# Router of a mixture-of-experts encoder layer: the four best by match-replace on padded rows, ranks offset in the rank matrix, gates and residual products at another place

## The reference, cut to what matters

```python
def moe_ffn(h, w_router, b_router, w_gu, b_gu, w_down, b_down):   # T = 256 tokens
    t = h.reshape(T, D)
    logits = (t @ w_router + b_router)                  # T x 32
    top_val, top_idx = lax.top_k(logits, 4)
    gates = jax.nn.softmax(top_val, axis=-1)
    ...                                                 # tokens sorted by expert
    def expert_block(args):                             # each expert over its tokens
        gu = xb @ w_gu[e] + b_gu[e]                     # 1024 -> 2048
        g, u = jnp.split(gu, 2, axis=-1)
        g = jnp.minimum(g, 7.0); u = jnp.clip(u, -7.0, 7.0)
        act = g * jax.nn.sigmoid(1.702 * g) * (u + 1.0)
        return act @ w_down[e] + b_down[e]              # 1024 -> 1024
    ...                                                 # times gate, summed by token
# reference: x = x + token_mixer(...); h = rmsnorm(x, norm2_g)
#            x = x + moe_ffn(h, ...);  return rmsnorm(x, final_g)
```

## Time and profile before

| | us |
|---|---|
| median of the runs | 1162.61 |
| lowest, highest | 1161.68, 1163.89 |
| the profiled execution, its time | 1161.16 |
| its span (first to last instruction) | 1159.4 |
| PE busy in it | 1085.6 (94%) |
| DVE busy in it | 378.7 (33%) |
| ACT busy in it | 233.7 (20%) |

### The profile page before, as it was taken

One profiled execution on the slowest core, in us unless ns is written; L12 is line 12 of the kernel. 1 busy time (PEld: TensorE's weight loads), 2 busy tenths in 40 slices (PEclk: granted clock), 3 DMA queues, 4 the chain that ended last, 5 costly groups with the idle time before them and its releaser, 6 DMA issues.

```text
span 1159.4 us, 13119 instructions
## 1 busy us (share of the span) xinstructions
PE 1085.6 (94%) x5379; PEld 497.7 (43%) x5379; DVE 378.7 (33%) x669; ACT 233.7 (20%) x370; POOL 0.2 (0%) x4
## 2 busy tenths in 40 slices
PE   5998999999999999999998989898989898999987
PEld 5997889833333333333333323333333333323332
DVE  6996798533122221222212121221221212112112
ACT  5388853110111111111101111111110101011102
POOL 0000000000000000000000000000000000000000
PEclk9999999989999999999999999999999999999999
DMA  8543236999999999999999999999999999999996
GB/s 351 186 173 142 77 132 278 419 407 382 423 384 429 427 426 430 428 428 430 427 430 427 428 430 428 429 428 427 430 427 428 430 428 430 428 427 428 428 427 262
DMA packets 33054, 439.95 MB, mean 379 GB/s; under 512 B 3808, under 2 KB 3936, under 8 KB 6272
## 3 DMA queue, kind: packets, MB, share of 16 engines
q1 hardware_dynamic: 32544, 438.53, 90.1%
q10 hardware_dynamic: 480, 0.99, 0.2%
HBM read 438.46 MB, written 1.05 MB: 379 GB/s over the span
## 4 chain that ended last, share of the span: by engine, by line
PE 62%; DMA 31%; DVE 3%; SPq 2%; ACT 1%; issue 1%; DVEq 0%
DMA slot<-in_w_gu_dram 26%; PE ps L1343 25%; PE ps L1047 12%; PE ps L1352 10%; DMA slot<-in_w_down_dram 5%; PE ps L1315 5%; PE ps L1296 3%; PE ps L1401 2%; SPq L352 2%; PE ps L1310 1%; PE ps L1102 1%; DVE slot_r L631 1%; PE ps L1145 1%; PE ps L1274 1%; PE ps L1166 1%
## 5 line engine op out<-in xcount | busy, mean ns | idle before, releaser
L1343 PE MATMUL ps<-slot,lru 128*64 128x512 f32 x880 | 198.5, 595 | 20.6 <-DMA slot<-in_w_gu_dram 20.2
L1352 PE MATMUL ps<-slot,lru 128*64 128x512 f32 x896 | 208.3, 600 | 7.3 <-DMA slot<-in_w_down_dram 7.1
L1343 PE MATMUL ps<-slot,qT 128*64 128x512 f32 x880 | 200.4, 597 | 14.0 <-DMA slot<-in_w_gu_dram 14.0
L992 DVE COPY lru<-ps 128x512 f32<-128x512 f32 x32 | 22.1, 692 | 337.2 <-PE ps L1343 337.2
L1343 PEld LDWEIGHTS ps<-slot,lru 128*64 128x64 f32 x880 | 63.0, 137 | 151.8 <-issue 113.8
L1343 PEld LDWEIGHTS ps<-slot,qT 128*64 128x64 f32 x880 | 61.3, 136 | 147.9 <-issue 133.2
L1352 PEld LDWEIGHTS ps<-slot,lru 128*64 128x64 f32 x896 | 57.8, 136 | 113.3 <-issue 92.6
L559 ACT ACTIVATE lru<-ps 128x512 f32<-128x512 f32 x32 | 19.1, 598 | 410.9 <-PE ps L1343 410.9
L975 DVE TENSOR_SCALAR lru<-sq,x_sb,small 128x64 f32<-128x64 f32 x64 | 17.2, 312 | 252.5 <-PE ps L1296 252.5
L1047 PE MATMUL ps<-wide_r,slot_r 128*128 128x256 f32 x492 | 66.2, 286 | 0.2 <-DVE slot_r L631 0.2
L1315 PE MATMUL ps<-lru 128*128 128x512 f32 x136 | 65.5, 605 | 0.9 <-DVE lru L1027 0.9
(11 more groups left out here) (213 smaller groups left out, 856.5 us busy)
## 6 DMA issues: line engine op xcount, KB each, us to landing
slot<-in_w_gu_dram SPq DMA_DIRECT2D x110, 2048.0 KB, 34.0
slot<-in_w_down_dram SPq DMA_DIRECT2D x54, 2048.0 KB, 33.6
wide<-in_w_gu_dram SPq DMA_DIRECT2D x15, 2048.0 KB, 34.5
slot<-in_pre_dram SPq DMA_DIRECT2D x14, 2048.0 KB, 8.2
wide<-in_w_down_dram SPq DMA_DIRECT2D x8, 2048.0 KB, 35.3
slot<-in_w_down_dram SPq DMA_DIRECT2D x8, 512.0 KB, 30.4
slot<-in_w_lru_dram SPq DMA_DIRECT2D x2, 1024.0 KB, 13.5
wide<-in_w_gu_dram SPq DMA_DIRECT2D x2, 1024.0 KB, 14.8
```

Of the source, the lines that this page charges most:

```text
L992: nc.vector.tensor_copy(gu_sb[:, 0:BANK], ps[:, 4, :]).then_inc(gu_v, 1)
L1343: ins = nc.tensor.matmul(ps[64 * side:64 * side + 64, 4 + b, :], xgT[i % 2][:, k, :], rows[r][:, o:o + BANK], start=(k == 0), stop=(k == K ...
L1352: ins = nc.tensor.matmul(ps[64 * side:64 * side + 64, bank, :], actT[(i - 1) % 2][:, k, :], w[:, r, side * BANK:(side + 1) * BANK], start= ...
```

## The change

- **Mask.** The logits have four more columns (`NL` = 36), which hold 3.0e38. The four largest values of a row are these, and the next four of the sorted eight (`top8[:, t, 4:8]`) are the chosen experts' logits. `match_replace` replaces all eight in a copy (`left`) by -3.0e38; the mask is where `left` differs from `logit`. This is the new `top_mask(t)`, which also makes the negative maximum. `top_experts(t)` keeps positions, floats and `hot`, and moves behind both tiles' ranks.
- **Ranks.** The first rank matrix is the upper-triangular ones minus 4096 times the identity, so the product has the offset in it; `first_ranks` is one addition and the selection matrix. The fill of `rank_col` with -1 moves up to where DVE waits for the mixer, and `rank_col` and `gate` have tiles of their own.
- **PE's order.** `residual_in_bank(0)` moves behind `gather_tile(1)`; `residual_in_bank(1)` moves behind `gathered_transposes(0)`; `ranks(0)` stands ahead of all of `logits(1)`; the gate transposes move into step 0, between `gate_up(0, 0, 0)` and `gather(1)`.
- **Gates.** The product with `hot` and its sum stand behind `scale_gathered(0, 0)`; one column block of gates is kept instead of five, and a step reads it at `n & 31`.

```diff
+NL = NE + TOPK
+HUGE = 3.0e38
...
-                nc.scalar.activation(ex4[:, t, :], top8[:, t, 0:TOPK], ACT.Exp, bias=nmax[:, t:t + 1],
+                nc.scalar.activation(ex4[:, t, :], top8[:, t, TOPK:2 * TOPK], ACT.Exp, bias=nmax[:, t:t + 1],
...
+            nc.vector.memset(logit[:, :, NE:NL], HUGE).then_inc(logits_padded, 1)
...
-            nc.vector.tensor_copy(tri[:, :, :], sq[:, 1:3, :]).then_inc(tri_ok, 1)
+            nc.vector.scalar_tensor_tensor(out=tri[:, 0, :], in0=ident, scalar=-FAR, in1=upper, op0=ALU.mult,
+                                           op1=ALU.add).then_inc(tri_ok, 1)
+            nc.vector.tensor_copy(tri[:, 1, :], ones).then_inc(tri_ok, 1)
+            dve.wait_ge(logits_padded, 1)
+            link(nc.vector.memset(rank_col[:, :, :], -1.0))
...
+            def top_mask(t):
+                link(nc.vector.match_replace(left[:, t, :], top8[:, t, :], logit[:, t, :], -HUGE))
+                nc.vector.tensor_tensor(mask_b[:, t, :], left[:, t, 0:NE], logit[:, t, 0:NE], ALU.not_equal
+                                        ).then_inc(mask_ok, 1)
+                nc.vector.tensor_scalar(nmax[:, t:t + 1], top8[:, t, TOPK:TOPK + 1], -1.0, None,
+                                        ALU.mult).then_inc(top_ok, 1)
...
             def top_experts(t):
                 link(nc.vector.max_index(idx_u[:, t, :], top8[:, t, :], logit[:, t, :]))
                 link(nc.vector.tensor_copy(idx_f[:, t, :], idx_u[:, t, :]))
                 link(nc.vector.tensor_tensor(hot[:, t], slotno[:, 0:NE].unsqueeze(1).to_broadcast(four),
-                                             idx_f[:, t, 0:TOPK].unsqueeze(2).to_broadcast(four), ALU.is_equal))
-                link(nc.vector.tensor_reduce(mask[:, t, :], hot[:, t].rearrange("p k e -> p e k"), AX.X, ALU.add))
-                nc.vector.tensor_copy(mask_b[:, t, :], mask[:, t, :]).then_inc(mask_ok, 1)
-                nc.vector.tensor_scalar(nmax[:, t:t + 1], top8[:, t, 0:1], -1.0, None, ALU.mult).then_inc(top_ok, 1)
+                                             idx_f[:, t, TOPK:2 * TOPK].unsqueeze(2).to_broadcast(four), ALU.is_equal))
...
             def first_ranks(t):
                 dve.wait_ge(rank_ps, t + 1)
-                link(nc.vector.scalar_tensor_tensor(out=ranked[:, t, :], in0=ps[:, 4 + t, 0:NE], scalar=FAR,
-                                                    in1=mask[:, t, :], op0=ALU.add, op1=ALU.mult))
-                link(nc.vector.tensor_scalar(rank_col[:, t, 0:NE], ranked[:, t, :], -FAR, None, ALU.add))
+                link(nc.vector.tensor_scalar(rank_col[:, t, 0:NE], ps[:, 4 + t, 0:NE], FAR, None, ALU.add))
...
             top_values(0)
+            top_mask(0)
             transposed_copy(1)
             inverse_variance(ssum[:, 1:2], T + 2)
-            link(nc.vector.memset(rank_col[:, :, :], -1.0))
-            top_experts(0)
             first_ranks(0)
             top_values(1)
-            top_experts(1)
+            top_mask(1)
             first_ranks(1)
+            for t in range(T):
+                top_experts(t)
...
             link(nc.vector.tensor_tensor(g4, ex4, einv.unsqueeze(2).to_broadcast([P, T, TOPK]), ALU.mult))
+            scale_gathered(0, 0)
             link(nc.vector.tensor_tensor(hotg, hot, g4.unsqueeze(3).to_broadcast([P, T, TOPK, NE]), ALU.mult))
-            link(nc.vector.tensor_reduce(gate, hotg.rearrange("p t k e -> p t e k"), AX.X, ALU.add))
-            nc.vector.tensor_copy(gate_col[:, :, 0:NE], gate).then_inc(mask_ok, 1)
...
-            scale_gathered(0, 0)
+            nc.vector.tensor_reduce(gate, hotg.rearrange("p t k e -> p t e k"), AX.X, ALU.add).then_inc(mask_ok, 1)
...
             for r in range(1, ROUNDS):
-                nc.vector.tensor_scalar(rank_col[:, :, r * NE:(r + 1) * NE], ranked, -FAR - CAP * r, None,
+                nc.vector.tensor_scalar(rank_col[:, :, r * NE:(r + 1) * NE], rank_col[:, :, 0:NE], -float(CAP * r), None,
                                         ALU.add).then_inc(cols_ok, 1)
-                nc.vector.tensor_copy(gate_col[:, :, r * NE:(r + 1) * NE], gate).then_inc(cols_ok, 1)
             dve.wait_ge(gateT_ps, 1)
...
+                e = column(n if isinstance(n, int) else n & (NE - 1))
                 for t in range(T):
                     nc.vector.tensor_scalar(sel_gate[:, t, o:o + CAP], slotno[:, 0:CAP], rank_col[:, t, column(n)],
-                                            gate_col[:, t, column(n)], ALU.is_equal, ALU.mult).then_inc(sgate_ok, 1)
+                                            gate[:, t, e], ALU.is_equal, ALU.mult).then_inc(sgate_ok, 1)
...
             second_transposes(1)
-            residual_in_bank(0)
-            logits(1, range(4))
             ranks(0)
-            logits(1, range(4, KD))
+            logits(1, range(KD))
...
                 gate_up(n, i, 0)
+                if first:
+                    gate_transposes()
                 if not last:
                     gather(n + 1)
...
             gather_tile(1).then_inc(xg_ps, 1)
+            residual_in_bank(0)
+            gathered_transposes(0)
             residual_in_bank(1)
-            gathered_transposes(0)
-            pe.wait_ge(mask_ok, T + 1)
-            for t in range(T):
-                ins = nc.tensor.transpose(ps[0:NE, 6, t * P:(t + 1) * P], gate[:, t, :], ident)
-            ins.then_inc(gateT_ps, 1)
             step(0, 0, True)
```

More of the change, by code:

```diff
@@ L144, in encoder_layer @@
         NCOL = (ROUNDS + 1) * NE
[L145 to L148, removed]
+        tflat = x_sb[:, 0, :]
+        rank_col = sb("rank_col", [P, T, NCOL])[:, :, :]
+        gate = sb("gate", [P, T, NE])[:, :, :]
+        logit = scratch(T * NL).rearrange("p (t e) -> p t e", t=T)
+        left = tflat[:, 640:640 + T * NL].rearrange("p (t e) -> p t e", t=T)
         top8 = tflat[:, 64:80].rearrange("p (t k) -> p t k", t=T)
@@ L155, in encoder_layer @@
         hotg = tflat[:, 384:640].rearrange("p (t k e) -> p t k e", t=T, k=TOPK)
-        mask = tflat[:, 640:704].rearrange("p (t e) -> p t e", t=T)
         mask_b = tflat[:, 835:867].bitcast(bf16).rearrange("p (t e) -> p t e", t=T)
-        gate = tflat[:, 704:768].rearrange("p (t e) -> p t e", t=T)
-        ranked = tflat[:, 768:832].rearrange("p (t e) -> p t e", t=T)
         cmax, rnd, rnd2 = tflat[0:1, 832:833], tflat[0:1, 833:834], tflat[0:1, 834:835]
@@ L892, in top_values @@
                 dve.wait_ge(rstd_ok, 2 + t)
-                link(nc.vector.scalar_tensor_tensor(out=logit[:, t, :], in0=ps[:, 4 + 2 * t, 0:NE],
+                link(nc.vector.scalar_tensor_tensor(out=logit[:, t, 0:NE], in0=ps[:, 4 + 2 * t, 0:NE],
                                                     scalar=rstd[:, t:t + 1], in1=brt[:, :], op0=ALU.mult, op1=ALU.add))
                 link(nc.vector.max(top8[:, t, :], logit[:, t, :]))
+            def top_mask(t):
[4 more added lines that the diff above has]
+                                        ALU.mult).then_inc(top_ok, 1)
             def top_experts(t):
@@ L900, in top_experts, with value, scale_gathered @@
                 link(nc.vector.tensor_tensor(hot[:, t], slotno[:, 0:NE].unsqueeze(1).to_broadcast(four),
[L901 to L904 removed]
+                                             idx_f[:, t, TOPK:2 * TOPK].unsqueeze(2).to_broadcast(four), ALU.is_equal))
             def first_ranks(t):
                 dve.wait_ge(rank_ps, t + 1)
[L908 to L910 removed]
+                link(nc.vector.tensor_scalar(rank_col[:, t, 0:NE], ps[:, 4 + t, 0:NE], FAR, None, ALU.add))
                 nc.vector.tensor_scalar(sel_next[:, t, :], slotno[:, 0:CAP], rank_col[:, t, 0:1], rstd[:, t:t + 1],
                                         ALU.is_equal, ALU.mult).then_inc(sel_ok, 1)
+            def value(v):
+                return v if isinstance(v, int) else dve.snap(v)
+            gain2 = cst[:, C_G2:C_G2 + KD].rearrange("p (h k) -> p k h", h=2)
+            def scale_gathered(n, i):
+                dve.wait_ge(xT_ps, value(n + 1))
+                nc.vector.tensor_tensor(xgT[i % 2].rearrange("p (h k) n -> p k h n", h=2),
+                                        ps[:, 7, :].rearrange("p (k h n) -> p k h n", k=KD // 2, h=2),
+                                        gain2.unsqueeze(3).to_broadcast([P, KD // 2, 2, CAP]),
+                                        ALU.mult).then_inc(xg_ok, 1)
             for n in range(3):
@@ L964, in _ @@
             nc.vector.tensor_copy(gateT, ps[0:NE, 6, 0:TOK].rearrange("p (t n) -> p t n", t=T)).then_inc(sg_ok, 2)
-            dve.wait_ge(cols_ok, 2 * (ROUNDS - 1))
+            dve.wait_ge(cols_ok, ROUNDS - 1)
+            dve.wait_ge(mask_ok, T + 1)
             def column(n):
@@ L1363, in down, with gate_transposes @@
                 ins.then_inc(chunk_used[4 + j], 1 + AHEAD if isinstance(n, int) and n == 1 else 1)
+            def gate_transposes():
+                pe.wait_ge(mask_ok, T + 1)
+                for t in range(T):
```

(2 more changed lines are left out.)

13 lines of the change are left out of this document (2 added, 11 removed).

## The result

| | before | after |
|---|---|---|
| median of 22 runs each, us | 1161.00 | 1163.57 |
| lowest and highest, us | 1158.50, 1164.48 | 1161.26, 1169.91 |
| profiled execution, its span, us | 1159.4 | 1162.8 |

The ratio of after to before is 1.0021, with a 95% interval of 1.0011 to 1.0031: the change costs 2.4 us (1.3 to 3.6). The forecast was 1163.6 us within 1161.1 to 1165.5, and "within 0.2%" with a chance of 79%. The time is the forecast one, but by luck, by two errors that cancel almost wholly: before is 1161.0 over 22 runs, not the 1162.6 of the three runs at hand, and the shift is 2.4 us, not 1.0. At 0.21% it lies just outside the 0.2%, and its interval of 0.11% to 0.31% reaches to both sides of that bound.

The account below looks back on a forecast made before the run. PE was taken to set the pace to 341.01 us, then the weight transfers; -1.55 + 0.91 + 1.34 + 0.35 = +1.05 us at `gather(1)` gave 1163.6 us on the median, range 1161.1 to 1165.5.

Parts of the forecast that it names:

- The frame: From step 0 to the issue at 341.01 PE sets the pace, then transfers; a `gather(1)` shift reaches the end unchanged.
- The mask's worth: Second tile, DVE line 893 to `gather_tile(1)`: shorter mask and ranks take 1.95 us in place of 3.10.
- `gather_tile(1)` starts 1.55 us earlier: In the router: earlier second-tile logits and the shorter mask start the second gather at 234.8 in place of 236.33.
- the clock term: Around the start of step 0: PEclk's low stretch stays where it was, step 0 starts further into it, 0.35 us more.
- the sign of a first `gate_up` that starts 0.4 to 1 us earlier: Start of step 0: a residual product directly ahead of `gate_up`, which starts that much before 241.96.
- The exposed residual product: Between the gathered transposes and the first `gate_up`: a residual product now stands there, 0.91 us more.
- The wait in step 0: Between the first `gate_up` and `gather(1)`: PE stands for gate transposes, DVE's copy and selection, 1.34 us.
- The sum: At `gather(1)` in step 0: -1.55 + 0.91 + 1.34 + 0.35 = +1.05 us, shifting the end alike.
- the second rival: In the router or step 0: more dense work at low clock, 3.3 us more of it, +2.7 in all, 1165.3; 15%.
- the first rival: In the router: shorter gaps keep the clock up, `gather(1)` comes 1.3 us earlier, 1161.3 us; 17%.
- The median to start from: Whole kernel before: the forecast started from 1162.6 us, the median of three runs that spread over 2.2 us.

Follow-up runs that it names:

- f: The kernel before with only the gate transposes moved into step 0, between the first `gate_up` and `gather(1)`; ratio to before 1.0014 (1.0005 to 1.0024).
- j: The kernel before with two unused 256-column products added in PE's stand-stills, ahead of `ranks(1)` and `gather_tile(1)`; ratio to before 0.9995 (0.9983 to 1.0007).
- e: The changed kernel with one unused residual-shaped product added between the second tile's transposes and `ranks(0)`; ratio to before 1.0001 (0.9986 to 1.0015).
- b: The changed kernel with PE's order of before and gates made ahead of the scaling, leaving the mask part; ratio to before 0.9988 (0.9978 to 0.9999).
- c: The changed kernel with both residual products back at their old places, gate transposes still in step 0; ratio to before 1.0007 (0.9994 to 1.0020).
- h: b with the first residual product cut in two halves, one between `ranks(1)` and the second gather; ratio to before 0.9973 (0.9959 to 0.9987).
- a: The changed kernel with DVE's `select(1)` ahead of the copy that waits for the gate transposes; ratio to before 1.0015 (1.0002 to 1.0028).
- d: The kernel before with only the residual products moved as in the change; ratio to before 1.0033 (1.0016 to 1.0050).

## Why the prediction was right, and where it was off

**The frame held.** PE sets the pace up to the issue at 341 us and the transfers behind it do from there on: a shift of `gather(1)` arrives in that issue unchanged, in all thirteen traces, and at the end of the span to 0.2 us in ten of them. The range held the time.

**The mask's worth held**: 1.95 us were worked out from DVE's line 893 to `gather_tile(1)`. In after it is 1.01 to the mask, 0.92 from `ranks(1)` (236.68) to 237.60, and 0.05 of signal, 1.98. The replacement took 0.18 us, as the search of the earlier trace rows. The prediction also set these rows against the Trainium skill, "VectorE: DVE Perf Modes", section on the TRN2 errata, and took from its table a fixed cost of 58 cycles. The text below that table says itself that the row under-predicts and that the measured fixed term is about 150 cycles. As an estimate from that figure 32 columns take 190 ns, and there the rows of 0.17 to 0.19 us agree.

**"`gather_tile(1)` starts 1.55 us earlier" failed.** From the start of the stretch it is 9.28 us after against 9.52 before: 0.24 earlier. The step that went wrong is the clock term: "if the low stretch stays where it was", 0.35 us. I took the low stretch to stay where it was, and so let the second tile's logits and `gather_tile(0)` run at full clock. They did not: the logits took 2.83 us from 232.02 in place of 1.9, about 0.9 more, and `gather_tile(0)` held up `ranks(1)` by 0.74 us, from 235.94 to 236.68. Against that, the logits began 0.3 us sooner than I had them. 1.55 - 0.9 - 0.74 + 0.3 is 0.21, the 0.24 within rounding. By this the sign of a first `gate_up` that starts 0.4 to 1 us earlier failed too: it starts 15.76 us into the stretch after against 15.15 before, 0.61 later.

**The exposed residual product** was put at 0.91 us. From `gather_tile(1)` to `gate_up` it is 5.63 us before and 6.48 after: 0.85.

**The wait in step 0** was put at 1.34 us, and in the change as a whole with 0.35 us of clock. From `gate_up` to `gather(1)` it is 3.73 before and 4.99 after: 1.26, since the clock was back sooner than I had it in after; f has 1.25 against the first profile of before and 1.50 against the second, whose `gate_up` ran at full clock as in f. The term is right to 0.2 us and the 0.35 us did not come.

**The sum**: -0.24 + 0.85 + 1.26 = +1.87 us in the profiles in place of +1.05, and 2.4 us (1.3 to 3.6) in the times. The difference is the clock. This is the second rival, which had 15%: it named an earlier fall, with the missing dense product as its cause, and had 3.3 us more of low clock, where 3.4 came. It put the price at 1.65 us over the forecast; against the forecast's own terms it took 0.8 us, since part of the low stretch lay over thin work and waits. I had used the cause as an argument against the first rival and not followed it through for the forecast; with both dense products gone from a stretch of transposes and 32-column logits it should have been the likeliest case.

The first rival rested in part on a misreading: "PE's longest stand-still, the one before 236.33" has 0.85 us, and the one ahead of `ranks(1)` at 235.22 has 1.00. Both shrink in after, and the clock falls earlier all the same.

The Trainium skill, "TensorE: Matmul & The Clock Gate", Part 4, which says that a transpose does not count as busy for the clock in the way that a matmul does, spoke for that rival. The trace does not contradict it, but no run here has transposes as the only difference. The same page's section "Why this matters for your kernels" advises against idle gaps between bursts of matmuls, and means longer ones than any in this router. Run j goes the way of the advice: it fills two of at most 1.0 us, and the low stretch is gone. But the rule as stated would let the clock stay up in after, where it fell behind stand-stills of 0.26 and 0.47 us; there the measurement decides.

**The median to start from** was off by 1.6 us. Three runs that spread over 2.2 us don't fix a median to better than that, and the forecast's absolute figure had the good luck of it. From 1161.0 us the same sum would have given 1162.05, 1.5 us below what was measured: still in the range, but the shift itself is more than twice the forecast one.

What stays open: whether the thin logits, the transposes or the stand-stills weigh most for the clock. e and j show that dense work in their place prevents the fall, not which of the three brings it about; nor do b and c, with one order up to the fall, show what decides between them. The change's own time lies 0.5 us above what its two profiles show against those of before, inside the interval.

## What to carry to other kernels

A matmul that seems to cost time in a latency-bound stretch may be what keeps TensorE's clock up. Before moving dense work out of a stretch, read the granted clock window by window and ask what stays there: here moving two products lengthened the stretch by 1.7 us or more, and adding a useless one shortened it by 2.2. Fill a stand-still with work that is due anyway, cut to its size, as h does; and when a step is moved ahead of a wait on another engine, look at what stands in that engine's queue between the answer and what the first engine needs next (a: the selection moved ahead of the copy took the 1.00 us of waiting away).

## What I had not expected of the hardware

- Products whose result nobody reads shorten a stretch: 18.88 to 17.25 us (j), 20.75 to 18.38 us (e), each with the granted clock at 1.00 throughout the stretch in place of 6.8 and 10.2 us at half.
- At half clock, 32-column matmuls with a full weight load slow down too: 1.08 us for eight at full and 1.90 at half clock (d).
- The clock also falls at some 100 to 110 us in some executions of one and the same kernel and not in others, and the router begins later then: at 228.32 us in the first profile of after, with 6.8 us of low clock ahead of it, and at 226.45 in the second, with none. The runs of before spread over 6 us, more than anything that the change did, and the longer ones have the lower mean clock: in the 32 that a to d were measured against, those at 0.993 took 1162.2 to 1164.2 us and those at 0.996 or more 1158.8 to 1162.9.
